# The shared expert of a two-layer mixture-of-experts kernel moves behind the ninth group of three experts

## What is computed

```python
scores = sigmoid(xf @ router_w)                  # 256 tokens, 64 experts
_, idx = top_k(scores + router_b, 6)
wts = sel / sum(sel) * 2.5                       # sel: scores of the six
# each chosen expert, for its tokens:
hid = silu(xb @ w_gate[e]) * (xb @ w_up[e])      # 1024 -> 256
y = (hid @ w_down[e]) * w                        # 256 -> 1024
shared = (silu(xf @ sh_gate) * (xf @ sh_up)) @ sh_down   # every token
return routed + shared
```

## Time and profile before

| what | us |
|---|---|
| median of 3 runs (1499.29 to 1504.4) | 1501.29 |
| profiled execution, its own time | 1497.9 |
| its span, first to last instruction | 1496.1 |
| TensorE busy (88% of the span) | 1320.8 |
| VectorE busy (42%) | 634.9 |
| ScalarE busy (20%) | 298.5 |
| moved by DMA | 502.79 MB, mean 336 GB/s |
| share of the chain that ended last: TensorE, DMA | 54%, 37% |

### The profile page before, as it was taken

How to read it: one execution, slowest core, us unless ns; L and a number is a source line. 1 busy time by engine, 2 the same in 40 slices (tenths; PEclk the granted TensorE clock), 3 DMA queues, 4 the chain that set the end, 5 groups by cost and what they waited for, 6 DMA issues and landing times.

```text
span 1496.1 us, 22046 instructions
## 1 busy us (share of the span) xinstructions
PE 1320.8 (88%) x9056; PEld 685.7 (46%) x9056; DVE 634.9 (42%) x1170; ACT 298.5 (20%) x501; POOL 66.7 (4%) x116
## 2 busy tenths in 40 slices
PE   4998778899998888897887999999999888898895
PEld 1444326764444333333436776875444333343342
DVE  5997733254433223222224788453433222322322
ACT  2236232311111111111112114031111111111110
POOL 0000681000000000000000000000000000000000
PEclk9999889999999999999997999989999999999998
DMA  9672963958999999999997870767999999999993
GB/s 381 238 180 71 188 262 126 396 219 322 420 423 421 423 423 423 423 423 423 422 423 230 303 297 29 303 245 267 380 424 424 421 425 421 421 424 423 422 423 130
DMA packets 59800, 502.79 MB, mean 336 GB/s; under 512 B 10348, under 2 KB 17260, under 8 KB 20588
## 3 DMA queue, kind: packets, MB, share of 16 engines
q1 hardware_dynamic: 59148, 499.19, 83.9%
q10 hardware_dynamic: 544, 2.10, 0.3%
HBM read 496.57 MB, written 4.69 MB: 335 GB/s over the span
## 4 chain that ended last, share of the span: by engine, by line
PE 54%; DMA 37%; DVE 4%; issue 2%; ACT 2%; SPq 1%; DVEq 0%; ACTq 0%
PE ps L678 50%; DMA arena<-in_w_experts 34%; DMA arena<-in_ada_w 3%; PE ps L407 2%; ACT arena L1278 1%; SPq L451 1%; PE ps L984 1%; DVE arena L1885 1%; PE ps L723 0%; ACT L1278 0%; DVE arena L1718 0%; PE ps L931 0%; DVE arena L1719 0%; DVE arena L1742 0%; DVE arena L1716 0%
## 5 line engine op out<-in xcount | busy, mean ns | idle before, releaser
L678 PE MATMUL ps<-arena 128*32 128x512 f32 (+12 forms) x8236 | 1235.1, 497 | 151.8 <-DMA arena<-in_w_experts 78.4
L678 PEld LDWEIGHTS ps<-arena 128*32 128x32 f32 (+6 forms) x8236 | 622.5, 132 | 749.2 <-issue 543.6
L1278 ACT ACTIVATE arena<-ps 128x512 f32<-128x512 f32 (+7 forms) x303 | 167.5, 553 | 928.9 <-PE ps L678 817.5
L1278 ACT ACTIVATE arena<-arena 128x256 f32<-128x256 f32 (+8 forms) x138 | 93.6, 700 | 171.5 <-DVE arena L1940 61.1
L1924 DVE SCALAR_TENSOR_TENSOR arena<-arena,ps 128x256 f32<-128x256 f32 x44 | 21.2, 481 | 234.1 <-ACT arena L1278 234.1
L1938 DVE CAST arena<-ps 128x512 bf16<-128x512 f32 x44 | 30.4, 692 | 175.0 <-PE ps L678 175.0
L1881 DVE COPY arena<-ps 128x512 f32<-128x512 f32 x44 | 30.4, 692 | 172.7 <-PE ps L678 172.7
L1914 DVE TENSOR_TENSOR arena<-arena 128x1024 bf16<-128x1024 f32 x44 | 53.9, 1226 | 39.5 <-ACT arena L1278 39.2
L1940 DVE TENSOR_TENSOR arena<-ps,arena 128x1024 f32<-128x1024 f32 x44 | 53.9, 1225 | 1.5
L668 POOL MEMSET arena<- 128x1 f32 x2 | 0.2, 101 | 1215.1 <-PE ps L984 1215.1
L984 PE MATMUL ps<-arena 128*128 128x128 f32 x352 | 52.8, 273 | 0.0
(11 more groups left out here) (225 smaller groups left out, 479.6 us busy)
## 6 DMA issues: line engine op xcount, KB each, us to landing
arena<-in_w_experts SPq DMA_DIRECT2D x118, 2048.0 KB, 28.0
arena<-in_w_experts SPq DMA_DIRECT2D x118, 1024.0 KB, 27.4
arena<-in_ada_w SPq DMA_DIRECT2D x40, 1024.0 KB, 6.5
arena<-in_w_experts SPq DMA_DIRECT2D x10, 3072.0 KB, 18.7
arena<-in_hy_w_in SPq DMA_DIRECT2D x6, 2048.0 KB, 12.0
arena<-in_ada_w SPq DMA_DIRECT2D x4, 2048.0 KB, 22.1
arena<-in_w_shared SPq DMA_DIRECT2D x2, 3072.0 KB, 10.5
arena<-in_hy_w_out SPq DMA_DIRECT2D x1, 4096.0 KB, 12.5
```

Of the source, the lines that this page charges most:

```text
L678: return pe.matmul(out, lhsT, rhs, start=start, stop=stop, skip_group_check=skip)
L1278: return act.activation(out, in_, func, **kw)
```

## The change

The shared expert is no longer among the early loads. Six experts are (FIXED = 6): 0 to 3 in columns 0 to 3, 4 in column 4 and 5 in column 7, the first of triple 1. The ring works in two halves, slots (0, 4, 5) and (1, 2, 3), which the triples use in turn (`parity`). After triple 8, the ninth, SP loads the shared expert into slot 1 once group 9 is done; triple 9 then follows in the half that triple 8 used, and triple 10 in the other, its last part behind the shared expert's products. TensorE multiplies the shared expert ahead of group 11 (SH_GROUP): two halves of gate-up, with the two halves of `to_tokens(10)` behind them; `shared_down` becomes the filler of group 11, and group 0 has none. The accumulators are opened by `to_tokens(0)`. Silu and product of the shared expert go in two halves through the GU bank, and `sgs` and `hTs` lie in `r_keep`.

```diff
-RING, FIRST_SLOT, SHARED = 6, 3, 2
+RING = 6
 STATIC = 4
-FIXED = STATIC + 1
+FIXED = STATIC + 2
...
+TRIPLES = NG - PAIRS
+SH_AFTER = 8
+SH_GROUP = PAIRS + SH_AFTER + 1
...
-sgs, hTs = at(m3, 2 * L), tiles(m3 + 2 * L, 2, L)
...
+sgs, hTs = tiles(r_keep, 2, L), tiles(r_keep + 2 * L, 2, L)
...
-def slot_of(e):
-    return (e + FIRST_SLOT) % RING
+def parity(t):
+    return t % 2 if t <= SH_AFTER else (t + 1) % 2
+HALVES = ((0, 4, 5), (1, 2, 3))
+SHARED = HALVES[(SH_AFTER + 1) % 2][0]
+def slot_of(c):
+    if c < STATIC:
+        return (4, 5, 2, 3)[c]
+    t, m = divmod(c - STATIC, 3)
+    return HALVES[parity(t)][m]
 def triple_loads(t, li):
-    fixed = li + 1 if t % 2 == 0 else 0
-    return 3 * (li * len(range(t % 2, NG - PAIRS, 2)) + t // 2 + 1) - fixed
+    def loads(last):
+        return sum((2 if i < 2 else 3) for i in range(last + 1) if parity(i) == parity(t))
+    return li * loads(TRIPLES - 1) + loads(t)
 TABLES = 1 + NSETS
...
     def first_experts(li, experts):
         for e in experts:
-            load(wring[:, slot_of(e)], A["w_experts"][li, e], f"w_pair{min(e // 2, 1)}")
+            c = e if e < FIXED - 1 else STATIC + 3
+            load(wring[:, slot_of(c)], A["w_experts"][li, e], f"w_pair{min(e // 2, 1)}")
...
-        first_experts(li, (3, 4))
+        first_experts(li, (4, 5))
...
         def half_loads(columns, experts, t, down):
-            part, name = (slice(GUW, WEXP), f"w_dn{t % 2}") if down else (slice(0, GUW), f"w_gu{t % 2}")
+            part, name = (slice(GUW, WEXP), f"w_dn{parity(t)}") if down else (slice(0, GUW), f"w_gu{parity(t)}")
             for c in columns:
-                if c - RING >= 0:
-                    sp.wait_ge(sem("dn_mm" if down else "gu_mm"), li * NG + group_of(c - RING) + 1)
-                elif down:
-                    sp.wait_ge(sem("sh_down"), li + 1)
+                m = (c - STATIC) % 3
+                if t == SH_AFTER + 2 and m == 0:
+                    sp.wait_ge(sem("sh_down" if down else "sh_gu"), li + 1 if down else 2 * (li + 1))
                 else:
-                    sp.wait_ge(sem("sh_gu"), 2 * (li + 1))
+                    before = t if t < PAIRS else PAIRS + t - (1 if t == SH_AFTER + 1 else 3 if t == SH_AFTER + 2 else 2)
+                    sp.wait_ge(sem("dn_mm" if down else "gu_mm"), li * NG + before + 1)
                 load(wring[:, slot_of(c), part], A["w_experts"][li, experts[c]][:, part], name)
         sp.wait_ge(sem("tables_ready"), TABLES * li + 1)
-        first = {c: expert_at(c) for c in range(FIXED, STATIC + 6)}
-        half_loads((5, 6), first, 0, False)
-        half_loads((7,), first, 1, False)
-        half_loads((5, 6), first, 0, True)
-        half_loads((7,), first, 1, True)
-        half_loads((8, 9), first, 1, False)
-        half_loads((8, 9), first, 1, True)
-        for t in range(2, NG - PAIRS):
-            triple = range(STATIC + 3 * t, STATIC + 3 * t + 3)
-            experts = {c: expert_at(c) for c in triple}
-            half_loads(triple, experts, t, False)
-            half_loads(triple, experts, t, True)
+        for t in range(TRIPLES):
+            c = STATIC + 3 * t
+            columns = (c + 1, c + 2) if t < 2 else (c + 1, c + 2, c) if t == SH_AFTER + 2 else (c, c + 1, c + 2)
+            experts = {i: expert_at(i) for i in columns}
+            half_loads(columns, experts, t, False)
+            half_loads(columns, experts, t, True)
+            if t == SH_AFTER:
+                sp.wait_ge(sem("dn_mm"), li * NG + PAIRS + t)
+                load(wring[:, SHARED], A["w_shared"][li], "w_shared")
...
     sp.wait_ge(sem("y_mm"), 1)
-    load(wring[:, SHARED], A["w_shared"][0], "w_shared")
+    first_experts(0, (2, 3))
+    sp.wait_ge(sem("ada_mm"), LATER)
     first_experts(0, (0,))
-    sp.wait_ge(sem("ada_mm"), LATER)
+    sp.wait_ge(sem("att_mm"), 1)
     first_experts(0, (1,))
-    sp.wait_ge(sem("att_mm"), 1)
-    first_experts(0, (2,))
     moe_loads(0)
...
-    load(wring[:, SHARED], A["w_shared"][1], "w_shared")
-    first_experts(1, range(3))
+    first_experts(1, range(4))
     moe_loads(1)
...
         def to_tokens(n, ks):
             for k in ks:
                 for s in range(3):
-                    last = mm(acc(k), yb[:, s, k * P:(k + 1) * P], oh[:, n % 2], False, n == NG - 1 and s == 2, skip=True)
+                    last = mm(acc(k), yb[:, s, k * P:(k + 1) * P], oh[:, n % 2], n == 0 and k % 2 == 0 and s == 0, n == NG - 1 and s == 2, skip=True)
             return last
...
             rows_turned(n)
-        pe.wait_ge(sem("w_shared"), 16 * (li + 1))
-        def shared_gate_up(c, ks=range(KD)):
-            for k in ks:
-                last = mm(ps[:, 6 + c // 2, (c % 2) * L:(c % 2 + 1) * L], gate_up(SHARED, k)[:, c * P:(c + 1) * P], hX[:, k], k == 0, k == KD - 1)
-            return last
+        def shared_gate_up(f):
+            for half in range(2):
+                for k in range(KD):
+                    a = half * FF + f * P
+                    last = mm(ps[:, GU, half * L:(half + 1) * L], gate_up(SHARED, k)[:, a:a + P], hX[:, k], k == 0, k == KD - 1)
+            last.then_inc(sem("sh_gu"), 1)
...
         def shared_down(k):
             for f in range(2):
-                last = mm(acc(k), w_down(SHARED, f, k // 4)[:, (k % 4) * P:(k % 4 + 1) * P], hTs[:, f], k % 2 == 0 and f == 0, False, skip=True)
+                last = mm(acc(k), w_down(SHARED, f, k // 4)[:, (k % 4) * P:(k % 4 + 1) * P], hTs[:, f], False, False, skip=True)
             return last
-        shared_gate_up(0)
         pe.wait_ge(sem("route"), 4 * li + 1)
...
         mm(ps[:, 0, 2 * NE:3 * NE], ones, m1_, False, True).then_inc(sem("route_mm"), 1)
-        shared_gate_up(1, range(0, 4))
         pe.wait_ge(sem("route"), 4 * li + 2)
         for t in range(2):
             last = pe.transpose(ps[:, 3, t * P:(t + 1) * P], unsorted[:, t], ident)
         last.then_inc(sem("hrow_mm"), 1)
-        shared_gate_up(1, range(4, KD)).then_inc(sem("sh_gu"), 1)
...
         mm(ps[0:1, 0, 3 * NE:4 * NE], extent, ident[:, 0:NE], True, True).then_inc(sem("route_mm"), 1)
-        shared_gate_up(2)
         pick_rows(0)
         find_tokens(0)
         turn_rows(0)
-        shared_gate_up(3).then_inc(sem("sh_gu"), 1)
         def filler(n, ks):
-            return to_tokens(n - 1, ks) if n >= 1 else [shared_down(k) for k in ks][-1]
+            if n == SH_GROUP:
+                return [shared_down(k) for k in ks][-1]
+            return to_tokens(n - 1, ks) if n >= 1 else None
+        def wait_rows(n):
+            pe.wait_ge(sem("oh_ready"), li * NG + n + 1)
+            pe.wait_ge(sem("y_dve"), 2 * (li * NG + n + 1))
         for n in range(NG):
             t = n - PAIRS
+            if n == SH_GROUP:
+                pe.wait_ge(sem("w_shared"), 16 * (li + 1))
+                pe.wait_ge(sem("h_done"), li * NG + n)
+                shared_gate_up(0)
+                wait_rows(n - 1)
+                to_tokens(n - 1, range(0, 4))
+                pe.wait_ge(sem("sh_hidden"), 2 * li + 1)
+                shared_gate_up(1)
+                to_tokens(n - 1, range(4, KD)).then_inc(sem("sc_mm"), 1)
+                pe.wait_ge(sem("sh_hidden"), 2 * (li + 1))
             if t < 0:
-                pe.wait_ge(sem(f"w_pair{n}"), 16 * (2, 3)[n] * (li + 1))
+                pe.wait_ge(sem(f"w_pair{n}"), 16 * (2, 4)[n] * (li + 1))
             else:
-                pe.wait_ge(sem(f"w_gu{t % 2}"), 16 * triple_loads(t, li))
+                pe.wait_ge(sem(f"w_gu{parity(t)}"), 16 * triple_loads(t, li))
             pe.wait_ge(sem("xt_act"), li * NG + n + 1)
             pe.wait_ge(sem("xt_dve"), li * NG + n + 1)
             if n >= 1:
                 pe.wait_ge(sem("h_done"), li * NG + n)
             gate_up_of(n).then_inc(sem("gu_mm"), 1)
-            if n == 0:
-                pe.wait_ge(sem("sh_hidden"), li + 1)
-            else:
-                pe.wait_ge(sem("oh_ready"), li * NG + n)
+            if n >= 1:
+                wait_rows(n - 1)
             filler(n, range(0, 4))
             if n + 1 < NG:
                 pick_rows(n + 1)
...
             if n + 1 < NG:
                 turn_rows(n + 1)
-            filler(n, range(6, KD)).then_inc(sem("sc_mm" if n >= 1 else "sh_down"), 1)
+            if n >= 1:
+                filler(n, range(6, KD)).then_inc(sem("sh_down" if n == SH_GROUP else "sc_mm"), 1)
             pe.wait_ge(sem("hT_ready"), li * NG + n + 1)
...
             if t >= 0:
-                pe.wait_ge(sem(f"w_dn{t % 2}"), 16 * triple_loads(t, li))
+                pe.wait_ge(sem(f"w_dn{parity(t)}"), 16 * triple_loads(t, li))
             down_of(n).then_inc(sem("dn_mm"), 1)
...
-        act.wait_ge(sem("sh_gu"), 2 * li + 1)
-        f(sgs, ps[:, 6, :], ACT.Silu).then_inc(sem("sh_sg"), 1)
...
         for n in range(NG):
+            if n == SH_GROUP:
+                for i in range(2):
+                    act.wait_ge(sem("sh_gu"), 2 * li + i + 1)
```

(15 more changed lines are left out.)

## The result

The change makes the kernel slower: 1505.1 us (median of 20 runs, 1499.9 to 1512.2) against 1499.5 us (20 runs, 1494.5 to 1504.4), a ratio of 1.0036 with a 95% interval of [1.0022, 1.0050]. The forecast was 1500.1 us and "no change"; on a base of 1499.5 the forecast gain of 1.2 us is a loss of 5.4 us. Rival C, the ring that runs dry amid the layer, had named the side and came near the size (1506), though not for the reason that it gave.

A forecast was written before the change was run, and what follows sets the result against it. Weight transfers bound each expert stage, ending with its last byte; per layer 8.4 us lead - 7.4 for the shared expert's bytes - 0.4 idle DMA = 0.6 us, 1.2 in two, from 1501.3 to 1500.1 us; range 1494.5 to 1506.

The forecast's parts named there:

- Rival C: Mid-layer: ring runs dry because shared gate-up or group 11 take longer than summed; -2.4 us a layer, 1506 us; chance 0.09.
- What bounds the kernel, and the bytes: Expert stage ends when its last byte has landed, plus an unchanged tail; both versions load the same bytes, priced at nothing.
- full stretch: Layer 0's stage from 374 us to layer end: transfers at 422 GB/s without pause; to start from about 365 us.
- lead: How much earlier TensorE reaches group 2: 3.0 + 5.4 = 8.4 us; less 7.4 leaves 1.0 us per layer.
- The front: Routing phase to group 0's gate-up: starts 3.0 us earlier, with low clock costing part; bounds 5.1 us and nothing.
- rival B: TensorE stays at 1.2 GHz from rank products into gate-up 0; 1509 us, milder forms 1504; together chance 0.17.
- rival A: Front: clock holds or returns with the rank products, so 5.1 us; 2.9 us a layer, 1495.5 us; chance 0.24.
- Group 0: First expert group, without shared down products as filler: 17.0 us instead of 22.4, so 5.4 us earlier.
- The term of 7.4: Cost in us of the shared expert's 3 MB, which now ride in the full stretch; subtracted from the lead.
- The middle: SP's waits around the shared expert, after triple 8: between nothing and 0.7 us of idle DMA a layer, taken as 0.4.
- T: Start of triple 8's (group 10's) gate-up; queue of 23 MB then reckoned at 56.9 us, shared down done T + 55.0 to 56.6.
- No gap in GB/s 57 us after group 10's gate-up began: Sign, mid-layer: transfers go on without a gap there; prediction wrong if GB/s falls in the middle.

The follow-up runs named there:

- e4: Changed kernel with 8 more products of 256 tokens, results unused, ahead of the second half of the shared gate-up; 1512.3 us, ratio 1.0079 to the kernel before.
- e3: Changed kernel with 16 unused products filling TensorE's idle stretches in the routing phase; 1501.5 us, ratio 1.0009 to the kernel before.
- e6: Changed kernel with the shared expert neither loaded nor multiplied (output lacks its term); 1482.7 us, ratio 0.9879 to the kernel before.
- e1: Changed kernel with all 16 shared down products ahead of group 11's gate-up instead of within the group; 1499.9 us, ratio 0.9997 to the kernel before.
- e2: Changed kernel with triple 10's last 1 MB down part issued behind triple 11's gate-up parts in SP's order; 1499.1 us, ratio 0.9993 to the kernel before.
- e9: The kernel of e2 run again on another chip; 1501.3 us against 1497.7 us for the kernel before, ratio 1.0019.
- e10: The kernel of e5 run once more; ratio 0.9987 to the kernel before.
- e11: Changed kernel with e2's load order and 22 idle products (9, 3, 5 and 5) in the routing phase; ratio 0.9983 to the kernel before.
- e5: Changed kernel with both e3's 16 idle products and e2's load order; ratio 0.9977 to the kernel before.
- e8: Changed kernel with both e3's 16 idle products and e1's order of the shared down products; ratio 0.9995 to the kernel before.
- e7: The changed kernel as it is, run again with a second profile; ratio 1.0039 to the kernel before.

## Why the prediction was wrong, point by point

- **What bounds the kernel, and the bytes**: right. Every slice from 377 us to the end of layer 0's stage has 422 to 424 GB/s, but the one with the gap, and what e4 adds without transfers counts about one for one. The full stretch is ahead nearly as said: TensorE's wait for group 9's weights ends 201.2 us after the router's products (498.62 - 297.39), 208.5 before, 7.3 us of lead; 7.4 in layer 1.

```profile
498.62 12.82 PE L688 MATMUL ps<-arena 128*32 128x512 f32 x92 [2.08 <-DMA arena<-in_w_experts]
```

```profile
502.21 12.83 PE L678 MATMUL ps<-arena 128*32 128x512 f32 x92 [1.72 <-DMA arena<-in_w_experts]
```

- **The front**: 3.0 us were forecast, with the clock low from the rank products until 3 us into the picking. Measured 2.4 and 2.0 us (27.3 and 27.9 after the router's products against 29.7 and 29.9), by that mechanism in the main: clock 0.50 from 310 to 320 us, and the picking took 5.6 us against 3.5, so about 4 of them at half rate. In layer 0 the rank products themselves still ran at 0.93; the order came 0.6 us later than before, and VectorE's chain had begun that much later already (6.2 against 5.7 us after the router's products). The "4 us of dense work" ahead of the clock's return, of rival B, were 2.9 and 3.0 us: full clock from 296.6 us, after a start at 293.73, and from 528.7 us, after one at 525.79. e3 shows the other end, 24.7 us, which is the 5.1 us of rival A to within 0.1. The Trainium skill ("TensorE: Matmul & The Clock Gate", section "What's actually happening") puts the ramp penalty at under 1% of a typical kernel span. Whoever prices it at nothing for that reason forecasts 1495.5 us here. By e3 it is small in the span here too (5 to 7 us of 1500 in the two fronts), which agrees, but it is as large as the whole effect.
- **Group 0**: 5.4 us forecast, 5.1 measured (22.4 before, 338.42 + 3.64 - 324.71 = 17.35 after). Layer 1 has 5.1 too (1031.59 + 3.64 - 1017.89 = 17.34 after, 22.45 before). Lead 7.5 and 7.1 instead of 8.4, which less 7.4 leaves nothing instead of 1.0 us a layer. The term of 7.4 itself measures 6.6 (e6 against e1, e2 and e9).
- **The middle is the step that failed**: "Against 56.9 that is between nothing and 0.7 us of idle DMA ... I take 0.4." It was 2.5 and 4.6 us. TensorE's side was right in layer 0, where the shared down products end at T + 56.0. In layer 1 they end at T + 57.2 (1270.60 + 1.8 - 1215.16), 0.6 us beyond the forecast's latest, since group 10's first stretch took 15.73 us at the low clock and not 14.52. Wrong in both layers was the DMA side, a queue that runs at full rate to T + 56.9 and then stops. From T to the end of the gap's first slices fewer bytes move than I let the queue hold, 23 units. An expert is 3 units and 3 x 1024 x 256 numbers of 4 bytes, so a unit is 1.049 MB and 23 are 24.1 MB:

```profile
520.87:574.00 53.13, 52.80 (x328) 0.97 1.01 423
574.00:576.00 2.00, 2.00 (x15) 1.00 0.81 336
576.00:578.00 2.00, 2.00 (x16) 1.00 0.44 139
```

  53.13 x 0.423 + 2 x 0.336 + 2 x 0.139 = 23.4 MB in layer 0, and 23.0 by the same sum up to 1272 us in layer 1. So 0.7 to 1.1 MB of later loads had already moved when TensorE started on triple 8's gate-up (whether ahead of that part's last byte or while its signal was on the way isn't shown), the rate falls from T + 53 to 54 on, and after the release it takes a slice or two to come back (270; 61 and 340). Those three together, about 2 us a layer, were missing from my sum, plus the cold start of group 10 and a T that came 1.5 us late in layer 1.
- **The margin.** I had a wait and a queue meet within 1 us and took the middle of my own error. Rival C had the place right ("decides from T + 56 on") and the price (3 us of idle transfers, 1506), and it got 0.09. Its reason, "because shared gate-up or group 11 take longer than summed", was not what happened: from group 10's end (537.59 + 3.64 in layer 0, 1233.10 + 3.64 in layer 1) to the last shared down product both layers took 35.7 us, where 36.2 were summed, and the queue was short. That its 1506 lies so near is in part luck. With the measured terms (lead 7.5 and 7.1, less 7.4, gap 2.5 and 4.6) the sum is -2.4 and -4.9 us, 7.3 in all. That is what the two stages of this execution lost (1.6 + 5.7), and more than the 5.4 of the medians.

As to the single marks: gate-up 0, group 1's lead (7.5 for 8 us), the low clock, and the stretch of TensorE without a wait after group 10 came as said. "No gap in GB/s 57 us after group 10's gate-up began" did not, and that was named as what would make the prediction wrong. The full stretch started 7.3 and 7.4 us earlier, on the edge of the other such sign ("under 7.4 us"), and layer 0's last group came 1.6 us later and not 0.6 earlier.

## What to carry to other kernels

Where a transfer queue is the bound, ask of every wait that the issuing engine meets how many us of queued transfers are left at that moment, and don't count on the last of them: its end is not sharp. Here a release had to come 3.0 to 4.8 us ahead of the reckoned end for nothing to be lost (reckoned end less release, plus what was missing, in the eight stages of the table; an estimate for this kernel). A load that waits for late work should stand behind those that don't: here one part of 1 MB, moved behind three others, or the awaited products moved ahead of one group, gave back 5 us on average (6 in e1 and e2, 2.5 in e9). And an early lead of TensorE buys only what it exceeds the bytes that were pushed into the full stretch for it: 7.1 to 7.5 us of lead for the 7.4 us of bytes reckoned is an even trade before any of its risks.

## What the runs showed of the hardware

- A queue of large loads doesn't run out at once. In the first slices of the gap the rate steps down (336, 139 GB/s; in layer 1 311, 49) instead of breaking off, and 0.7 to 1.1 MB of what was queued later had moved when TensorE started on an earlier load.
- In e3, e10 and e11 small idle products held the granted clock at 1.0 through a phase in which TensorE otherwise waits for VectorE; with the same 16 products it fell there in one layer of e5 (0.50 at 308 to 310 us), and in one layer of e8 just behind it (0.50 at 1006 to 1008 us). So their effect isn't the same in each execution.
- The changed kernel's runs spread over 12.3 us (1499.9 to 1512.2), those of the kernel before over 9.9. The length of the gap goes with the clock with which group 10 begins: 1.2 us missing where its first stretch took 12.83 us (e3, layer 0), 2.5 where it took 14.52, 3.6 and 4.9 where it took 15.59 and 15.73. It isn't the clock alone: with 14.52 again, e7's layer 1 misses 3.9. Whether this makes the spread isn't shown, since only one execution of each run was profiled.
